# A one-core Trainium2 layer kernel: x turned before its norm scale is known, the scale put on the products, and the first projection's weights loaded ahead of x's second half

## What is computed

```
h = concat([meta, x], axis=1)
hn = rms_norm(h, attn_norm_w)              # h * rsqrt(mean(h*h) + 1e-6) * w
proj = hn @ w_in
u_conv, q_lat, kv_lat, g_lin = split(proj) # 1024, 256, 128 + 32, 2048 columns
y_conv = conformer_conv(u_conv, ...)
y_mla = mla(q_lat, kv_lat, ...)            # kv_lat: latent c_kv (128) and rope key k_pe (32)
g = sigmoid(g_lin + gate_b)
h = h + (g0 * y_conv + g1 * y_mla) @ w_out
h = h + moe(rms_norm(h, ffn_norm_w), ...)  # top 4 of 32 experts, clamped SwiGLU
out = h[:, 16:]
```

## Time and profile before

| | us |
|---|---|
| median of 3 runs | 1117.16 |
| lowest and highest run | 1116.72, 1119.17 |
| span of the profiled execution | 1117.4 |

### The profile page before, as it was taken

One profiled execution on the slowest core, in us unless ns is written; L12 is line 12 of the kernel. 1 busy time (PEld: TensorE's weight loads), 2 busy tenths in 40 slices (PEclk: granted clock), 3 DMA queues, 4 the chain that ended last, 5 costly groups with the idle time before them and its releaser, 6 DMA issues.

```text
span 1117.4 us, 14726 instructions
## 1 busy us (share of the span) xinstructions
PE 1054.2 (94%) x6235; PEld 489.6 (44%) x6235; DVE 282.4 (25%) x717; ACT 156.2 (14%) x320; POOL 30.0 (3%) x31
## 2 busy tenths in 40 slices
PE   8999999999999999979999979889898997999997
PEld 7778875643333333333333333333233333333333
DVE  2698852561111111111111111112011111111111
ACT  3453351410000000000000000000000000000011
POOL 1000062000000000000000000000000000000000
PEclk8999999999999999999999989999999998999999
DMA  9933298799999999999999999999999999999996
GB/s 286 328 105 116 92 318 356 261 414 432 431 430 431 435 432 433 432 433 433 434 440 425 441 434 432 432 423 440 439 427 439 420 443 422 430 430 429 426 426 269
DMA packets 42271, 432.88 MB, mean 387 GB/s; under 512 B 3811, under 2 KB 22574, under 8 KB 28190
## 3 DMA queue, kind: packets, MB, share of 16 engines
q1 hardware_dynamic: 41918, 432.30, 92.7%
q0 software_dynamic: 160, 0.04, 0.1%
q10 hardware_dynamic: 160, 0.07, 0.0%
HBM read 431.35 MB, written 1.05 MB: 387 GB/s over the span
## 4 chain that ended last, share of the span: by engine, by line
PE 65%; DMA 32%; ACT 1%; DVE 1%; issue 1%; SPq 0%; ACTq 0%
DMA arena<-in_w_gate_up 32%; PE psum L972 27%; PE psum L1009 13%; PE psum L761 5%; PE psum L665 4%; PE psum L935 3%; PE psum L841 2%; PE psum L814 2%; PE psum L1019 2%; PE psum L989 1%; PE psum L944 1%; PE psum L994 1%; ACT arena L1379 1%; PE psum L752 1%; PE psum L726 0%
## 5 line engine op out<-in xcount | busy, mean ns | idle before, releaser
L972 PE MATMUL psum<-arena 128*64 128x512 f32 x2048 | 460.6, 607 | 40.7 <-DMA arena<-in_w_gate_up 32.0
L972 PEld LDWEIGHTS psum<-arena 128*64 128x64 f32 x2048 | 152.6, 140 | 342.5 <-issue 314.3
L1009 PE MATMUL psum<-arena 128*64 128x512 f32 x992 | 218.4, 592 | 0.0
L1698 DVE TENSOR_SCALAR arena<-psum 128x512 f32<-128x512 f32 x32 | 22.2, 692 | 722.9 <-PE psum L972 718.2
L1009 PEld LDWEIGHTS psum<-arena 128*64 128x64 f32 x992 | 69.3, 137 | 128.1 <-issue 124.4
L1366 ACT COPY arena<-psum 128x256 f32<-128x256 f32 x32 | 11.9, 373 | 553.7 <-PE psum L944 553.7
L1019 PE MATMUL psum<-arena 64*128 64x512 f32 x248 | 61.6, 614 | 6.8 <-ACT arena L1379 6.8
L761 PE MATMUL psum<-arena 128*128 128x256 f32 x256 | 59.0, 380 | 0.3 <-ACT arena L1261 0.3
L1379 ACT COPY arena<-psum 128x512 f32<-128x512 f32 x31 | 18.2, 587 | 238.5 <-PE psum L1009 238.5
L761 PEld LDWEIGHTS psum<-arena 128*128 128x128 f32 x256 | 47.7, 190 | 8.0 <-issue 1.2
L935 PE MATMUL psum<-arena 128*128 128x64 bf16 x1488 | 48.8, 191 | 2.2
(11 more groups left out here) (240 smaller groups left out, 572.6 us busy)
## 6 DMA issues: line engine op xcount, KB each, us to landing
arena<-in_w_down SPq DMA_DIRECT2D x26, 4096.0 KB, 30.9
arena<-in_w_gate_up SPq DMA_DIRECT2D x20, 4096.0 KB, 32.8
arena<-in_w_gate_up SPq DMA_DIRECT2D x18, 2048.0 KB, 18.3
arena<-in_w_down SPq DMA_DIRECT2D x8, 2048.0 KB, 25.6
arena<-in_w_gate_up SPq DMA_DIRECT2D x11, 1024.0 KB, 8.4
arena<-in_w_in SPq DMA_DIRECT2D x9, 1024.0 KB, 6.2
arena<-in_w_down SPq DMA_DIRECT2D x6, 1024.0 KB, 8.8
arena<-in_w_in SPq DMA_DIRECT2D x8, 512.0 KB, 8.6
```

The lines of the kernel that those rows point to most:

```text
L972: last = mm(b[64 * half:64 * half + 64, :], xe[i][:, k, :], channels(slot_gu[slot][:, j, o:o + FF], half), start=(k == 0 and first), stop= ...
L1009: last = mm(b[64 * c:64 * c + 64, :], aT[:, j, 64 * h:64 * h + 64], slot_dn[slot][:, j, c * 512:(c + 1) * 512], start=False, stop=(h == DC ...
L1698: ts(g_s, G, LIMIT, None, ALU.min).then_inc(S.g_ready, 1)
```

## The change

- SP loads the kv piece in two parts (channels 0 to 511 with `in_win[0]`, 512 to 1023 with `in_kv`) behind x tile 0 and ahead of x tile 1.
- PE turns h as it lands, waiting for `in_x` alone. DVE does all five weight multiplications (`turned_in`), now into a new buffer `rawT` that lies in pw2's later place. ACT's share (`HN_ACT`) is gone, and so are the five scalings in place.
- PE projects latent and rope key from `rawT`, in pieces: latent of columns 0 to 143, then the scale row for them, then the turns of x tile 1, then the rope key of columns 0 to 143, then four of the latent's matmuls for columns 144 to 271, the second scale row, and the rest.
- The scale row: DVE writes the reciprocal root on a diagonal (`diag`, identity times scale), and PE multiplies a matrix of ones by it, so that every partition holds the row. DVE copies it out (`rs_row`) and multiplies `rawT` by it into `hnT` in two instructions (`scaled`). q and everything after it read `hnT` as before.
- DVE then multiplies latent and rope key by the same row out of PSUM; ACT's two copies are gone. ACT's squaring of the latent waits for `ckv_ready`.
- POOL sets `ones_early`, and its four small loads of k and q norm weights now come behind the wait for `par_ready`.

```diff
     for i, job in enumerate(HN):
-        add(job, 1 + i, "hn_act" if job == HN_ACT else "hn_ready", ...)
+        add(job, 1 + i, "raw_ready", i + 1)
...
+    for i in range(2):
+        add(("rs", i), i, "rs_ready", i + 1)
...
             sp.dma_start(xpos[0:META, 2, :], a["meta_tokens"]).then_inc(in_x[2], 16)
-            for t in range(2):
-                sp.dma_start(xpos[:, t, :], x[t * P:(t + 1) * P, :]).then_inc(in_x[t], 16)
+            sp.dma_start(xpos[:, 0, :], x[0:P, :]).then_inc(in_x[0], 16)
+            for half, landed in ((0, in_win[0]), (1, in_kv)):
+                src = w_in.rearrange("(k p) c -> p k c", p=P)[:, 4 * half:4 * half + 4, COL_KV:COL_KV + KVL + ROPE]
+                sp.dma_start(win[0][:, 4 * half:4 * half + 4, 0:KVL + ROPE], src).then_inc(landed, 16)
+            sp.dma_start(xpos[:, 1, :], x[P:2 * P, :]).then_inc(in_x[1], 16)
...
-                pe.wait_ge(S.xs_ready, i + 1)
+                pe.wait_ge(in_x[t], 16)
...
+            for job in HN[0:3]:
+                turn_rows(job)
+            ckv = fill("ckv")
+            pe.wait_ge(in_win[0], 16)
+            pe.wait_ge(S.raw_ready, 3)
+            latent(ckv, 0, META + P, 0, 4)
+            pe.wait_ge(in_kv, 16)
+            latent(ckv, 0, META + P, 4, KD)
+            pe.wait_ge(S.diag_ready, 2)
+            pe.wait_ge(S.cols_clear, 4)
+            b = fill(("rs", 0))
+            mm(b[:, 0:META], ones_early[0:META, :], diag[0:META, 2, 0:META], start=True, stop=True)
+            filled(("rs", 0), mm(b[:, META:META + P], ones_early, diag[:, 0, :], start=True, stop=True))
+            for job in HN[3:5]:
+                turn_rows(job)
+            kpe = fill("kpe")
+            rope_key(kpe, 0, META + P)
+            pe.wait_ge(S.raw_ready, 5)
+            latent(ckv, META + P, P, 0, 4)
+            pe.wait_ge(S.diag_ready, 3)
+            filled(("rs", 1), mm(fill(("rs", 1))[:, 0:P], ones_early, diag[:, 1, :], start=True, stop=True))
+            filled("ckv", latent(ckv, META + P, P, 4, KD))
+            filled("kpe", rope_key(kpe, META + P, P))
...
             b = fill("q")
+            pe.wait_ge(S.hn_ready, 2)
...
+            def row_scales(i, t):
+                r = TR[t]
+                dve.wait_ge(S.xroot_ready, i + 1)
+                link(nc.vector.reciprocal(rsx[:, t:t + 1], rsx[:, t:t + 1]))
+                ts(diag[0:r, t, 0:r], ident[0:r, 0:r], rsx[0:r, t:t + 1], None, ALU.mult).then_inc(S.diag_ready, 1)
+
+            def scaled(i):
+                at = slice(META + P, L) if i else slice(0, META + P)
+                n = at.stop - at.start
+                nc.vector.tensor_copy(rs_row[:, at], full(("rs", i))[:, 0:n]).then_inc(S.rs_ready, 1)
+                dve.wait_ge(S.rs_ready, i + 1)
+                dve.wait_ge(S.raw_ready, 5 if i else 3)
+                tt(hnT[:, :, at], rawT[:, :, at], rs_row[:, at].unsqueeze(1).to_broadcast([P, KD, n]), ALU.mult
+                   ).then_inc(S.hn_ready, 1)
...
+            for job in HN[0:3]:
                 turned_in(job)
+            row_scales(0, 2)
+            row_scales(1, 0)
+            for job in HN[3:5]:
+                turned_in(job)
+            row_scales(2, 1)
+            scaled(0)
+            scaled(1)
+            tt(ckvn, full("ckv")[:, 0:L], rs_row, ALU.mult).then_inc(S.ckv_ready, 1)
+            tt(kpeT, full("kpe")[:, 0:L], rs_row, ALU.mult).then_inc(S.kpe_ready, 1)
```

More of the change, by code:

```diff
@@ L89 @@
 HN = [("hn", 2, 0), ("hn", 0, 0), ("hn", 0, 1), ("hn", 1, 0), ("hn", 1, 1)]
-HN_ACT = ("hn", 0, 1)
-HN_DVE = [job for job in HN if job != HN_ACT]
 OUT_PARTS = [(0, 0, 512), (0, 512, 512), (1, 0, 512), (1, 512, 384), (1, 896, 128)]
@@ L248, in layer @@
         assert at <= A0 + 3 * CHUNK
+        rawT = grid(D0 + 4096, KD, L)
         wo = grid(D0, 4, D)
@@ L262, in layer @@
         rsb2 = words(B0 + 6272 + L, SEQ)
+        rs_row = words(B0 + 6272, L)
         at = B0 + 8192
@@ L292, in layer @@
         assert at <= W0 + W
-        idle = words(WB, SEQ)
+        idle, ones_early, diag = words(WB, SEQ), words(WB + SEQ, P), grid(WB + SEQ + P, 3, P)
         hT = grid(WB, KD, P)
@@ L359, in layer @@
         in_win = [sem(f"in_win{s}") for s in range(RING)]
+        in_kv = sem("in_kv")
         in_wqb, in_wkvb, in_wo, in_pw2 = sem("in_wqb"), sem("in_wkvb"), sem("in_wo"), sem("in_pw2")
@@ L367, in layer @@
         in_early = {k: sem(f"in_early{k}") for k in list(EARLY) + ALONE}
-        for name in ("cols_clear pads_clear zero_clear pa_ready par_ready hn_act meta_ready xss_ready xroot_ready xs_ready hn_ready "
+        for name in ("cols_clear pads_clear zero_clear pa_ready par_ready meta_ready xss_ready xroot_ready raw_ready diag_ready rs_ready hn_ready ckv_ready "
                      "squares kpe_ready lvar_ready lroot_ready lat_ready csig_ready convin_ready v_ready "
@@ L423, in load_win @@
                     sp.dma_start(win[slot][:, :, to:to + n], src[:, :, frm:frm + n]).then_inc(in_win[slot], 16)
-            for i in range(2):
-                load_win(i)
+            load_win(1)
             for src, row, n in [("conv_dw_b", R_DWB, 4), ("conv_ln_w", R_LNW, 4),
@@ L584, in _ @@
             nc.gpsimd.memset(idle, 0.0).then_inc(S.cols_clear, 1)
+            nc.gpsimd.memset(ones_early, 1.0).then_inc(S.cols_clear, 1)
+            nc.gpsimd.memset(hc[:, :, 0:PAD], 0.0).then_inc(S.pads_clear, 1)
+            pool.wait_ge(S.par_ready, 1)
             with nc.allow_non_contiguous_dma(reason="one value a partition"):
@@ L591, in _ @@
                                ).then_inc(in_cols, 16)
-            nc.gpsimd.memset(hc[:, :, 0:PAD], 0.0).then_inc(S.pads_clear, 1)
-            pool.wait_ge(S.par_ready, 1)
             nc.gpsimd.memset(kk[:, 2, :], 0.0).then_inc(S.pads_clear, 1)
@@ L647, in _, with turn_rows @@
             filled("pa", nc.tensor.transpose(fill("pa")[:, 0:KD], rows[R_ATTN:R_ATTN + KD, 0, :], ident[0:KD, 0:KD]))
-            for i, job in enumerate(HN):
+            def turn_rows(job):
                 _, t, c = job
                 r = TR[t]
-                pe.wait_ge(S.xs_ready, i + 1)
+                pe.wait_ge(in_x[t], 16)
                 b = fill(job)
@@ L667, in project, with latent, rope_key @@
                 return last
[L669 to L680, removed]
+            def latent(b, n0, n, first, last):
+                for k in range(first, last):
+                    ins = mm(b[:, n0:n0 + n], win[0][:, k, 0:P], rawT[:, k, n0:n0 + n], start=(k == 0),
+                             stop=(k == KD - 1))
+                return ins
+            def rope_key(b, n0, n):
+                for k in range(KD):
+                    g = k % 4
+                    ins = mm(b[ROPE * g:ROPE * (g + 1), n0:n0 + n], win[0][:, k, P:P + ROPE], rawT[:, k, n0:n0 + n],
+                             start=(k < 4), stop=(k >= 4))
+                return ins
+            for job in HN[0:3]:
[21 more added lines that the diff above has]
+            filled("kpe", rope_key(kpe, META + P, P))
             pe.wait_ge(in_rows, 16 * 8)
@@ L1195, in _ @@
                 f(rsx[:, t:t + 1], ssx[:, t:t + 1], ACT.Sqrt, scale=1.0 / D, bias=eps).then_inc(S.xroot_ready, 1)
[L1196 to L1206, removed]
+            act.wait_ge(S.ckv_ready, 1)
+            f(sqk, ckvn, ACT.Square).then_inc(S.squares, 1)
             b = full("par")
@@ L1429, in full @@
                 return psum[:, bank, :]
[L1432 to L1438, removed]
             def turned_in(job):
@@ L1444, in turned_in @@
                 w = par[:, R_ATTN + 4 * c:R_ATTN + 4 * c + n].unsqueeze(2).to_broadcast([P, n, r])
[L1445 removed]
+                tt(rawT[:, 4 * c:4 * c + n, places(t)], b, w, ALU.mult).then_inc(S.raw_ready, 1)
+            def row_scales(i, t):
[11 more added lines that the diff above has]
+                   ).then_inc(S.hn_ready, 1)
             dve.wait_ge(S.cols_clear, 3)
@@ L1450, in _ @@
                                            ALU.add, ssx[0:META, 2:3]).then_inc(S.meta_ready, 1)
-            scaled(0, 2)
-            scaled(1, 0)
             nc.vector.tensor_copy(par[:, R_ATTN:R_ATTN + KD], full("pa")[:, 0:KD]).then_inc(S.pa_ready, 1)
             dve.wait_ge(S.pa_ready, 1)
[L1455 to L1458, removed]
+            for job in HN[0:3]:
                 turned_in(job)
+            row_scales(0, 2)
[7 more added lines that the diff above has]
+            tt(kpeT, full("kpe")[:, 0:L], rs_row, ALU.mult).then_inc(S.kpe_ready, 1)
             dve.wait_ge(S.par_ready, 1)
@@ L1486, in _ @@
             conv_in(0)
+            dve.wait_ge(S.kpe_ready, 1)
             ts(rsb, full("ssk")[:, 0:L], 1.0 / KVL, EPS, ALU.mult, ALU.add).then_inc(S.lvar_ready, 1)
```

1 line of the change is left out of this document (removed).

## The result

The change makes the kernel slower: 1128.40 us, median of 4 runs (1127.14 to 1129.92), against 1116.94 us before (4 runs, 1115.58 to 1119.17). The ratio is 1.0103, 95% interval 1.0088 to 1.0119: 11.5 us where 0.7 us were to be won. The prediction was wrong, in sign and in range.

A forecast was written before the change was run, and what follows sets the result against it. PE's gapless work from 18.2 us, then the experts' weight stream that starts when PE gets there, was taken as the bound; q at 17.5 instead of 18.22 wins 0.7 us from median 1117.16: 1116.4, range 1114.0 to 1118.6 (8 in 10).

The forecast's parts named there:

- The same kernel runs behind: After the changed front, everything was taken to run as before, so the 0.7 us won at q's start reaches the end.
- All lie beside PE's gapless stretch and cost nothing: Behind q's start: ACT's later squaring, `par_ready` near 19 us and POOL's work some 2 us later were priced at nothing.
- I take it that the clock falls as before: TensorE's clock at the front: half rate from about 8.3 to 12.1 us, with the latent taking 3.9 us.
- the first latent: PE's latent product for columns 0 to 143: start 8.05, 3.9 us at half clock, end about 11.95.
- Scale row: PE's two small matmuls after the first latent: between 0.2 and 0.6 us, taken as 0.35, to 12.3.
- The DVE chain: DVE's products, reciprocal, diagonal, copies and `scaled` before q, called the new wait; ends at 17.5 us, together with PE.
- Tile 1's landing: x tile 1's load, now behind the kv halves, lands at the latest at 10.2 us, before its turns.
- Rival D: x tile 1 lands late behind 1024 small rows, at 13.5 us, costing 1.2 us: 1117.6; chance 0.06.
- The second half-clock stretch: Half clock at 209.8 to 213 us, about 1.6 us lost; may move or vanish, so 1.6 either way.
- Rival C: Clock not back by 12.1 us; half rate reaches tile 1's turns and q: 2.6 us slower, 1119.8; chance 0.10.
- A: Rival: clock stays full through the front, q starts at 15.6 us, 2.6 us won: 1114.6; chance 0.22.
- B: Rival: the experts' weight stream hides the front's gain, nothing arrives at the end: 1117.2; chance 0.15.

The follow-up runs named there:

- e7: The kernel before with TensorE's experts' loop pinned to slot 104 of a 256-instruction fetch block; 1116.94 us.
- e8: The kernel before with TensorE's experts' loop pinned to slot 111 of a 256-instruction fetch block; 1126.00 us.
- e5: The changed kernel with a prefetch hint for the closing branch of TensorE's experts' loop, nothing moved; 1118.40 us.
- e1: The changed kernel with TensorE's experts' loop pinned to slot 0 of a 256-instruction fetch block; 1118.56 us.
- e12: The changed kernel with the prefetch hint and a reordered front: tile 1's turns, scale rows and first rope-key part earlier, tile 1's scale row early; 1118.84 us.
- e3: The kernel before with TensorE's experts' loop pinned to slot 0 of a 256-instruction fetch block; 1120.36 us.
- e10: e6 with the old order of loads, x's two tiles first; 1119.06 us.
- e6: The changed kernel, no pin or hint, with 40 TensorE instructions fewer ahead of the experts' loop; 1117.95 us.

## Why the prediction was wrong

*"The same kernel runs behind"*, *"All lie beside PE's gapless stretch and cost nothing"*: this is the step that failed, and it carries 9 to 10 of the 11.5 us (medians: 9.1 from e7 to e8, 10.0 from e5 to the changed kernel). Each added matmul was priced by its duration (0.35 us for the scale row) and at nothing for being there. As code it moved the loop across the end of a block. Neither the range nor any rival had a mechanism for it, though the rows for it were in the profile of before: 25 packets, none between 350 and 900 us while a loop of 1684 instructions turned, which says that the loop stayed resident. How near the edge it was, only a count of its instructions says.

*"I take it that the clock falls as before"* failed too: in the profile of before it was full from 4.80 to 8.21 and then half to 15.04, in that of the changed kernel half up to 14.26. Nor does it fall "for certain" where turns follow the weight's turn: in e1 it stayed full. Tile 0's turns were to end at 7.06 at full clock; at half rate they ended at 8.34 (2.91 us for 1.76). So the first latent started at 9.21 for 8.05. Its duration was right (4.18 for 3.9), and its end, 13.39, was 1.4 late. Scale row: 1.05 us to tile 1's turns for 0.35, and 0.65 in e1 at full clock, so this term was too small at either rate. Tile 1's turns 1.03 at full clock, as priced (1.09).

*The DVE chain*, the new wait, was right to the hundredth in its large terms, `scaled` with 1.36 and 1.23 us, and the copies took 0.30 and 0.28 for 0.25 and 0.23. But its start was late by the two errors above, and PE arrived with it (DVE at 19.75, PE's parameters at 19.6), so q came at 19.85 for 17.5. That both would arrive together was said and held; e12 shows that freeing DVE gives 0.8 us of q and no better median.

*Tile 1's landing*: in use at 8.48, inside "at the latest at 10.2". Rival D did not happen.

*The second half-clock stretch* was given no direction, 1.6 us either way. In the changed kernel's profile it is gone, and the front's 1.6 us of lag is gone with it. That is not the change's doing: the stretch is there in some executions and not in others, absent in e3, e7 and e8 with the old front and 10.2 us long in e5 and e10 with the new one. Their profiled executions are the longest of their ten, 1123.15 and 1124.34 us. In e5 the first expert group takes 9.39 us for 7.09:

```profile
215.13 9.39 PE L1006 MATMUL psum<-arena 128*64 128x512 f32 x32
```

Had the loop stayed resident, e5 and e6 say that the changed kernel would stand at 1118, inside the range and above the 1116.4.

*Rival C* gave the front 2.6 us, and it is 2.2 at low rate, but that is luck: C let the half rate reach into tile 1's turns and q, and both ran at full clock (1.03 us for 1.97). The half rate lay ahead of them, from the start on. *A* is e1's execution: it said q at 15.6 and 1114.6; measured 16.18 and 1115.24. *B* is refuted, since the spans follow the experts' start one for one (last column of the table). So the rate, which I had as one forecast and two rivals, differs from execution to execution of like fronts, and what sets it is open.

*The profiled execution's time* was taken as its span. The time lies 1.6 to 2.0 us above the span in all runs here, so the profiled execution of before was the one of 1119.17 us, with the experts at 213.94, where e3, e7 and e8 give 211.6 to 212.0: 0.5 to 0.6 us of that by q's start and 1.6 by the second half-clock stretch. Comparing the new front with that row flattered the change by 2 us.

## To carry to other kernels

Code ahead of a loop has a price that no instruction's duration shows: before adding to it, compare the instruction packets of the profile inside and outside the loop, and count how far the body is from one more block. If it is near the edge, arm the back edge's prefetch hint (e5), cut instructions elsewhere, or pin the head, and look at the loop's entry after a pin. And read the rate of a stretch from the duration of a known matmul, over several executions, before a microsecond at the start is promised.

## What the runs showed of the hardware

- A TensorE loop of 1684 instructions stays resident with its head at slot 104 and is fetched whole again, 9 packets a return, at slot 111: 25 against 61 packets, 903.4 against 913.1 us behind the experts' start.
- The first return that missed cost 6.26 (changed kernel) and 6.64 us (e8) of idle TensorE. The Trainium skill's Runtime: NRT & Kernel Launch (Instruction fetch mechanics) says that crossing a block is mostly hidden, and also that the instruction memory is only two cache lines. In the kernel before no packet is fetched from 350 to 900 us, over four returns of a loop of seven blocks, which rules two out for TensorE.
- What a refetch costs depends on the wait that stands at the loop's head anyway: 6.6 us at the first return, where weights were there; at the second a wait of 5.51 us became one of 4.53.
- With the hint, a body that touches eight blocks is fetched once: 25 packets for 61 (e5).
- After 6.6 us of idleness TensorE came back at clock 0.50, which cost some 2.9 us on top (e8).
- The clock column reads 1.00 ahead of the first clock record: up to 14.26 us in the changed kernel, where 16 records of 144 columns took 4.18 us, and 2.20 at full rate in e1.
